# Prompt attention: the scores of four and more key blocks spread over two PSUM banks, the keys' low part through half of the array's rows

## The reference

```python
def window_attend(q, k, v, pos_q, pos_k):
    s = jnp.einsum('...qgrd,...kgd->...qgrk', q, k).astype(jnp.float32) * SCALE
    dpos = pos_q[..., :, None] - pos_k[..., None, :]
    mask = (dpos >= 0) & (dpos < WINDOW) & (pos_k[..., None, :] >= 0)
    s = jnp.where(mask[..., :, None, None, :], s, NEG)
    p = jax.nn.softmax(s, axis=-1)
    return jnp.einsum('...qgrk,...kgd->...qgrd', p.astype(v.dtype), v)
...
        o_cmp, p = cmp_attend(nq, kc, vc, pos_p)
        idx, ok = select_blocks(p, pos_p)
        o_sel = sel_prompt(nq, sk, sv, idx, ok)
        o_win = window_prompt(nq, wk, wv)
        xp = finish(xp, retention_out(ro, rg, ret_gn_w[l]), nsa_combine(gates, o_cmp, o_sel, o_win), *tail)
```

## Time and profile before

| what | value |
|---|---|
| median of 3 runs | 1860.34 us |
| lowest, highest | 1859.66, 1862.49 us |
| profiled execution, its own time | 1858.16 us |
| span of that execution | 1856.3 us |
| PE busy | 1711.2 us (92%) |
| DVE, ACT, POOL busy | 845.9, 619.5, 137.1 us |
| attention of the prompt, on TensorE | about 667 to 968 us of the span |

### The profile page before, as it was taken

How to read it: one execution, slowest core, us unless ns; L and a number is a source line. 1 busy time by engine, 2 the same in 40 slices (tenths; PEclk the granted TensorE clock), 3 DMA queues, 4 the chain that set the end, 5 groups by cost and what they waited for, 6 DMA issues and landing times. The chain is left out here.

```text
span 1856.3 us, 29581 instructions
## 1 busy us (share of the span) xinstructions
PE 1711.2 (92%) x11649; PEld 1516.0 (82%) x11649; DVE 845.9 (46%) x1612; ACT 619.5 (33%) x1193; POOL 137.1 (7%) x236
## 2 busy tenths in 40 slices
PE   3999999994899669999989999999999999999897
PEld 2989989994784555555549889999999999999897
DVE  4466352132016356767876675322332233233366
ACT  5223322210011136666655554201320232023243
POOL 1000000004243300000000110000000000000000
PEclk8999999997899779999999999999999999999899
DMA  7111111125876510000007533211111111111544
GB/s 274 48 47 47 35 47 41 46 57 122 212 211 174 154 29 1 1 1 1 1 17 219 172 117 92 69 46 47 46 46 46 46 52 52 46 46 46 159 132 142
DMA packets 215436, 147.93 MB, mean 80 GB/s; under 512 B 13213, under 2 KB 205090, under 8 KB 214978
## 3 DMA queue, kind: packets, MB, share of 16 engines
q1 hardware_dynamic: 179970, 98.33, 18.8%
q0 software_dynamic: 12288, 37.21, 6.4%
q10 hardware_dynamic: 23040, 10.50, 2.2%
HBM read 133.71 MB, written 16.47 MB: 81 GB/s over the span
## 5 line engine op out<-in xcount | busy, mean ns | idle before, releaser
L1977 PE MATMUL psum<-act_hi,whi 128*128 128x344 f32 x960 | 310.4, 323 | 8.9 <-DVE wlo L2096 5.6
L1977 PE MATMUL psum<-act_hi,wlo 128*128 128x344 f32 x960 | 307.6, 320 | 0.0
L1977 PE MATMUL psum<-act_lo,whi 128*128 128x344 f32 x960 | 307.6, 320 | 0.0
L2096 DVE TENSOR_TENSOR wlo<-wraw,whi 128x1024 fp32r<-128x1024 f32 x111 | 136.0, 1226 | 264.5 <-ACT whi L1993 264.3
L1977 PE MATMUL psum<-hidden_hi,whi 128*128 128x344 f32 x768 | 247.3, 322 | 8.7 <-issue 8.7
L1977 PE MATMUL psum<-hidden_lo,whi 128*128 128x344 f32 x768 | 245.9, 320 | 0.0
L1977 PE MATMUL psum<-hidden_hi,wlo 128*128 128x344 f32 x768 | 245.9, 320 | 0.0
L1993 ACT ACTIVATE whi<-wraw 128x1024 fp32r<-128x1024 f32 x111 | 117.3, 1057 | 349.6 <-PE psum L1977 333.1
L231 PE MATMUL psum<-act_hi,whi 128*128 128x344 f32 x648 | 214.1, 330 | 8.9 <-DVE wlo L263 8.9
L231 PE MATMUL psum<-act_hi,wlo 128*128 128x344 f32 x648 | 207.6, 320 | 0.0
L231 PE MATMUL psum<-act_lo,whi 128*128 128x344 f32 x648 | 207.5, 320 | 0.0
(11 more groups left out here) (369 smaller groups left out, 2473.0 us busy)
## 6 DMA issues: line engine op xcount, KB each, us to landing
wraw<-in_w_down SPq DMA_DIRECT2D x48, 512.0 KB, 3.6
wraw<-in_w_up SPq DMA_DIRECT2D x40, 512.0 KB, 4.0
wraw<-in_w_in SPq DMA_DIRECT2D x27, 512.0 KB, 3.6
wraw<-in_w_o SPq DMA_DIRECT2D x23, 512.0 KB, 4.1
h_features<-mixed_then_h POOLq DMA_DIRECT2D x24, 172.0 KB, 2.4
h_again<-h_features POOLq DMA_DIRECT2D x3, 1376.0 KB, 11.3
x_rows<-in_x_prompt SPq DMA_DIRECT2D x4, 1024.0 KB, 9.6
dec_pages<-in_cache_sel_k SPq DMA_DIRECT2D x64, 64.0 KB, 3.0
```

Source lines behind the costliest of these rows:

```text
L1977: last = pe.matmul(ps[:, u % 3, 0:TN], wt[:, kt, :], xt[:, kt, cols], start=(kt == 0 and i == 0), stop=(kt == KT - 1 and i == 2))
L2096: dve.tensor_tensor(m.wlo[p % 2][:], wraw[raw_slot[p]][:], m.whi[p % 2][:].bitcast(F32), ALU.subtract).then_inc(lo_ready, 1)
```

## The change

Window blocks and selected blocks are treated alike by a new `keys`. With four or more key blocks, the first half of them (rounded up) goes to the end of the first bank, the rest to the start of the second, so that they still lie side by side for the readers (`spare`, `scores`). The high keys go through all 128 rows, once for each bank. The low keys go through 64 rows: bank one through rows 0 to 63, bank two through rows 64 to 127, with the queries' high part alone. The product of the two low parts is thus left out there. As `q_split` has the high part in only one half, `q_other` holds it in the other; GpSimd copies it, twice for each query block. With one to three key blocks nothing changes. In the window of five blocks the oldest and the newest block are taken together as the second bank's part, so one bf16 product of 256 columns adds both masks.

```diff
-        self.causal_bf = self.place("causal_bf", [P, P], BF16, o + 1536)
-        self.winlow_bf = self.place("winlow_bf", [P, P], BF16, o + 1792)
+        self.edges_bf = self.place("window_edges_bf", [P, 2 * P], BF16, o + 1536)
+        self.winlow_bf, self.causal_bf = self.edges_bf[:, 0:P], self.edges_bf[:, P:2 * P]
...
+        q_other = [m.place(f"att_q_other{i}", [P, NH // 2, P], F32R, m.A + 67584 if i else m.stage + 8192) for i in range(2)]
...
+        def window_order(i):
+            lo, hi = window(i)
+            return [lo + 1, lo + 2, lo + 3, lo, lo + 4] if i >= KW - 1 else list(range(lo, hi))
+        def in_first(blocks):
+            return (blocks + 1) // 2 if blocks >= 4 else blocks
+        def spare(blocks):
+            return (4 - in_first(blocks)) * P if blocks >= 4 else 0
+        def scores(bank, blocks):
+            at = spare(blocks)
+            return ps[:, bank:bank + 2, :].rearrange("p a n -> p (a n)")[:, at:at + blocks * P]
...
-            def keys(bank, g, a, w, hi, lo, q):
-                for n, k in enumerate((hi, lo)):
-                    if w == P:
-                        last = pe.matmul(ps[:, bank, 0:2 * P].rearrange("p (a n) -> p a n", n=P), q,
-                                         k[:, g, a:a + P].unsqueeze(1).broadcast_to([P, 2, P]), start=(n == 0), stop=(n == 1))
-                    else:
-                        last = pe.matmul(ps[:, bank, 0:w], q, k[:, g, a:a + w], start=(n == 0), stop=(n == 1))
-                return last
...
+            def keys(bank, g, order, hi, lo, i, h):
+                q, n = q_split[i % 2][:, h // 2, h % 2, :], len(order)
...
+                else:
+                    first = in_first(n)
+                    parts = order[:first], order[first:]
+                    outs = [c.rearrange("p (a n) -> p a n", n=P) for c in (ps[:, bank, (4 - first) * P:4 * P], ps[:, bank + 1, 0:(n - first) * P])]
+                    for part, out in zip(parts, outs):
+                        pe.matmul(out, q, blocks_of(hi[:, g, :], part), start=True, stop=False)
+                    for e, (part, out) in enumerate(zip(parts, outs)):
+                        rows = slice(e * HD, (e + 1) * HD)
+                        q_hi_part = q_split[i % 2][rows, h // 2, e, :] if e == h % 2 else q_other[i % 2][rows, h // 2, :]
+                        pe.matmul(out, q_hi_part, blocks_of(lo[rows, g, :], part), start=False, stop=True)
...
+                    pe.wait_ge(q_moved, 2 * ORDER.index(i) + 2)
...
+                keys(2, g, window_order(i), win_hi, win_lo, i, h)
+                if i >= KW - 1:
+                    last = pe.matmul(ps[:, 3, 0:2 * P], m.ident_bf[:], m.edges_bf[:], start=False, stop=True, skip_group_check=True)
...
+        @block.gpsimd
+        def _(pool):
+            for n, i in enumerate(ORDER):
+                for e in range(2):
+                    rows, other = slice(e * HD, (e + 1) * HD), slice((1 - e) * HD, (2 - e) * HD)
+                    pool.wait_ge(q_hi, 2 * n + e + 1)
+                    pool.tensor_copy(q_other[i % 2][other], q_split[i % 2][rows, :, e, :]).then_inc(q_moved, 1)
```

More of the change, by code:

```diff
@@ new lines, in keys @@
+            def keys(bank, g, order, hi, lo, i, h):
+                q, n = q_split[i % 2][:, h // 2, h % 2, :], len(order)
+                if n == 1:
+                    out = ps[:, bank, 0:2 * P].rearrange("p (a n) -> p a n", n=P)
+                    for x, k in enumerate((hi, lo)):
+                        pe.matmul(out, q, k[:, g, order[0] * P:(order[0] + 1) * P].unsqueeze(1).broadcast_to([P, 2, P]), start=(x == 0), stop=(x == 1))
+                elif n < 4:
+                    out = ps[:, bank, 0:n * P].rearrange("p (a n) -> p a n", n=P)
+                    for x, k in enumerate((hi, lo)):
+                        pe.matmul(out, q, blocks_of(k[:, g, :], order), start=(x == 0), stop=(x == 1))
+                else:
[8 more added lines that the diff above has]
+                        pe.matmul(out, q_hi_part, blocks_of(lo[rows, g, :], part), start=False, stop=True)
@@ L1457, in sel_keys, with at_block @@
+            def at_block(bank, x, n):
+                x += spare(n) // P
+                return ps[:, bank + x // 4, (x % 4) * P:(x % 4 + 1) * P]
             def sel_keys(k):
@@ L1459, in sel_keys @@
                 h = g * R + r
-                q = q_split[i % 2][:, h // 2, h % 2, :]
                 if g == 0 and r == 0:
                     pe.wait_ge(q_lo, 2 * ORDER.index(i) + 2)
+                    pe.wait_ge(q_moved, 2 * ORDER.index(i) + 2)
                 if k:
                     pe.wait_ge(exps, 2 * k - 1)
-                for a in range(0, (i + 1) * P, 512):
-                    keys(a // 512, g, a, min(512, (i + 1) * P - a), sel_hi, sel_lo, q)
-                pe.matmul(ps[:, i // 4, (i % 4) * P:(i % 4 + 1) * P], m.ident_bf[:], m.causal_bf[:], start=False, stop=True,
+                keys(0, g, list(range(i + 1)), sel_hi, sel_lo, i, h)
+                pe.matmul(at_block(0, i, i + 1), m.ident_bf[:], m.causal_bf[:], start=False, stop=True,
                           skip_group_check=True).then_inc(sel_scores, 1)
@@ L1474, in group_blocks @@
                     pe.matmul(ps[:, 3, 256 + x * CP:256 + (x + 1) * CP], q_split[i % 2][:, h // 2, h % 2, :].bitcast(F32), m.kcpT[:, g, :],
-                              start=(i < KW - 1 and x == 0), stop=True, skip_group_check=True)
+                              start=(i < 3 and x == 0), stop=True, skip_group_check=True)
                 return pe.matmul(ps[:, 3, 256:256 + R * CP].rearrange("p (a n) -> p a n", n=CP), m.ident_bf[:],
@@ L1486, in other_keys @@
                     pe.wait_ge(blk_steps, 4 * (k // R) + 2)
[L1487 to L1495, removed]
+                keys(2, g, window_order(i), win_hi, win_lo, i, h)
+                if i >= KW - 1:
+                    last = pe.matmul(ps[:, 3, 0:2 * P], m.ident_bf[:], m.edges_bf[:], start=False, stop=True, skip_group_check=True)
+                else:
+                    last = pe.matmul(at_block(2, i, i + 1), m.ident_bf[:], m.causal_bf[:], start=False, stop=True, skip_group_check=True)
                 if r == 0:
@@ L1522, in output @@
                 n = i + 1 + min(i + 1, KW)
-                lo, _ = window(i)
+                order = window_order(i)
                 if part == 0:
@@ L1535, in output @@
                         x = y - 1
-                        v = m.sv_tok[:, x, rows] if x <= i else m.wv_tok[:, lo + x - i - 1, rows]
+                        v = m.sv_tok[:, x, rows] if x <= i else m.wv_tok[:, order[x - i - 1], rows]
                         last = pe.matmul(out[x % 2], v, pT[grp % 2][:, x, :, :], start=(x == 0), stop=(x >= n - 2))
@@ L1585, in _ @@
                     w = (i + 1) * P
-                    act.activation(p[k % 3][:, 0:w], ps[:, 0:2, :].rearrange("p a n -> p (a n)")[:, 0:w], ACT.Exp,
+                    act.activation(p[k % 3][:, 0:w], scores(0, i + 1), ACT.Exp,
                                    bias=c[:, 1:2], accum_out=c[:, 4:5]).then_inc(exps, 1)
@@ L1591, in _ @@
                     w = min(i + 1, KW) * P
-                    act.activation(p[k % 3][:, SEQ:SEQ + w], ps[:, 2:4, :].rearrange("p a n -> p (a n)")[:, 0:w], ACT.Exp,
+                    act.activation(p[k % 3][:, SEQ:SEQ + w], scores(2, min(i + 1, KW)), ACT.Exp,
                                    bias=c[:, 2:3], accum_out=c[:, 5:6]).then_inc(exps, 1)
@@ L1656, in _ @@
                         dve.wait_ge(scaled, 2 * (k - 2))
-                    dve.tensor_reduce(c[:, 1:2], ps[:, 0:2, :].rearrange("p a n -> p (a n)")[:, 0:(i + 1) * P], AX.X, ALU.max, negate=True).then_inc(maxima, 1)
+                    dve.tensor_reduce(c[:, 1:2], scores(0, i + 1), AX.X, ALU.max, negate=True).then_inc(maxima, 1)
                 if 1 <= k <= len(steps):
@@ L1679, in _ @@
                     dve.wait_ge(win_scores, k + 1)
-                    dve.tensor_reduce(c[:, 2:3], ps[:, 2:4, :].rearrange("p a n -> p (a n)")[:, 0:min(i + 1, KW) * P], AX.X, ALU.max, negate=True).then_inc(maxima, 1)
+                    dve.tensor_reduce(c[:, 2:3], scores(2, min(i + 1, KW)), AX.X, ALU.max, negate=True).then_inc(maxima, 1)
                     if r == 0:
```

7 lines of the change are left out of this document (6 added, 1 removed).

## The result

The changed kernel takes 1868.93 us (median of 6 runs, 1865.86 to 1870.24), the kernel before in the same comparison 1862.37 us (6 runs, 1859.66 to 1864.47). The ratio is 1.0034, 95% interval [1.0021, 1.0047]: slower by 0.34%, some 6.3 us. The forecast was 1865.6 us, slower by 0.28%, range 1857 to 1871. It was built on 1860.34 us for the kernel before, the median of its first three runs; on the 1862.37 us of all six, the same sum would have given 1867.7 us.

The account below looks back on a forecast made before the run. PE was taken to bound the kernel; +4.7 us on PE (selected scores +4.0, window -0.8 and +1.4) and +0.6 for copies made +5.3 on 1860.34, so 1865.6 us, range 1857 to 1871.

Parts of the forecast that it names:

- PE bounds the attention: Attention: PE sets the pace, busy 132.88 of 139.08 us in query blocks 6 to 4; nearly every nanosecond moves the end.
- rival 4: Blocks 7 to 4: PE's waits for ACT absorb 2.6 us of the selected scores' growth; 1863.0 us, chance 0.11.
- do not absorb what is added ahead: Attention: PE's 32 waits for ACT, 11.0 us, start with the transposes and move along with them.
- The halves run together: Score routine: two low products of 64 rows run side by side, the pair costing what its wider half costs.
- rival 3: Score routine: halves run one after the other, +11.4 us more; 1877.0 us, chance 0.07.
- A call pays 0.29: Score routine: changing to half rows and back costs 0.09 + 0.10 + 0.09, plus 0.01, us a call.
- Rival 1: Score routine: the array's shape changes for nothing, 80 calls save 23.2 us; 1842.4 us, chance 0.10.
- rival 2: Score routine: the low pair's load is hidden, only drains cost, 8.0 us less; 1857.6 us, chance 0.08.
- The net by number of blocks: Score calls, net: 8 blocks +0.055, 7 +0.115, 6 +0.105, 5 +0.05, 4 +0.18 us; window of five -0.025.
- The masks: Window, 32 steps: old mask and bared load go, -0.04 - 0.085 us; the wider mask adds +0.05.
- GpSimd's copies: Sixteen copies: fourteen hidden, the first two delay PE's start by 0 to 1.2 us, taken as +0.6.
- their slack hides a copy that delays DVE later: Attention after the start: slack of DVE and ACT hides later copies, so these cost nothing.

Follow-up runs that it names:

- e4: The changed kernel, but both low products of a call go through rows 0 to 63; 1879.86 us, ratio to the kernel before 1.0097.
- e5: The kernel before, plus one product of 64 rows and 64 columns in each of 64 steps, ahead of the window's last mask; 1878.15 us, ratio 1.0087.
- e6: The kernel before, plus one product of 64 columns through all 128 rows in each of 64 steps, same place; 1862.42 us, ratio 1.0003.
- e3: The changed kernel, reordered: low pair first in the selected scores, last after the mask in the window; 1863.13 us, ratio to the kernel before 1.0012.
- e7: The changed kernel with low keys through all 128 rows, no copies, and the oldest block's mask between high and low products; 1857.19 us, ratio 0.9979.
- e1: The changed kernel, but low keys through all 128 rows and no GpSimd copies; 1855.14 us, ratio to the kernel before 0.9966.
- e2: The changed kernel, but four key blocks go as before, in one bank; 1864.88 us, ratio to the kernel before 1.0020.
- e8: The changed kernel with low keys through all 128 rows and no copies, run a second time; 1852.09 us, ratio to the kernel before 0.9955.

## Why the prediction was right

- **PE bounds the attention.** Right. What was added to PE arrived at the end, block by block. PE's wait for the banks of transposes fell from 11.0 us in 32 places to 9.2 in 31, which looks like the sign of rival 4. But by blocks nearly all of the fall (4.19 to 2.63 us) lies in block 7, where the two profiles differ in clock. In blocks 6 and 5 the wait is the same, before and then changed:

```profile
PE psum L1508 <- ACT att_pT L1572: 4.0, 16, 0.3
PE psum L1541 <- ACT att_pT L1613: 4.0, 16, 0.3
```

  So rival 4 is out for blocks 6 and 5. It isn't quite out below them: the forecast's sentence that these waits "do not absorb what is added ahead" fails in four steps of blocks 4 and 3, for 0.35 us together.

- **The halves run together.** Right, by e4; rival 3 is out.
- **A call pays 0.29.** Right: 0.26 to 0.29 in e5 against e6, and 0.09 + 0.20 in the timeline. Rival 1 (nothing) and rival 2 (drains alone, 0.19) are out. The format makes no difference that shows: L538 is fp32 and gave 0.09 and 0.10, the products here are `fp32r`. (For the way back the forecast set 0.43 for a pair of outputs where its own working gives 0.45, so its rows gave 0.07 and not 0.09; e3 finds 0.08.)
- **The net by number of blocks.** Nearly right. At 7 and 6 selected blocks the sum was met within 0.06 us a block. At block 4 it was 0.17 too high and at block 3 0.36 too high. Two things are missing in it. In the two steps of a block in which compressed scores follow the window's mask, the window's scores gain 0.07 to 0.08 us and not the 0.025 forecast: the wider mask costs nothing there. And a part is absorbed ahead of the transposes: in block 4 PE's wait ahead of them shrinks by 0.05 in the second and in the sixth step, in block 3 by 0.09 in the second, and in its fifth step the stretch of the transposes is 0.16 shorter. That fifth step grows from 4.29 to 4.45 us only, where the others of block 3 grow by 0.27 to 0.36.
- **The masks.** Right, and the more interesting half of the change: -0.125 + 0.05 a step, 0.08 to 0.09 by e7.
- **GpSimd's copies.** The forecast's step that failed is "their slack hides a copy that delays DVE later". The size of the first part was right: PE waits 5.80 us for its start and not 5.03, +0.77 where +0.6 was taken, because DVE and POOL stretch each other (DVE's two subtractions take 1.70 us, 1.40 in the earlier trace rows). The rows are from the timeline of the start:

```profile
665.65 1.70 DVE L1645 TENSOR_TENSOR att_q_split<-nqT,att_q_split 64x512 fp32r<-64x512 f32 x2 [0.32 <-ACT att_q_split L1600]
665.68 2.15 POOL L1592 CAST att_q_other<-att_q_split 64x512 fp32r<-64x512 f32 x2 [19.32 <-ACT att_q_split L1600]
667.97 0.77 PE L1486 MATMUL psum<-sel_kT_hi,att_q_split 128*128 128x512 f32 x1 [5.80 <-POOL att_q_other L1592]
```

  But in block 2, where a step is short, a copy also reaches PE: 0.4 us, and nothing had been forecast. In block 1 it is 0.2 more. DVE and POOL in block 2, and what PE waits for two steps later:

```profile
901.66 1.28 POOL L1592 CAST att_q_other<-att_q_split 64x512 fp32r<-64x512 f32 x2 [33.41 <-ACT att_q_split L1600]
```

```profile
902.33 0.83 DVE L1710 TENSOR_SCALAR att_p<-att_p,att_columns 128x384 f32<-128x384 f32 x1
903.08 0.40 DVE L1712 TENSOR_SCALAR att_p<-att_p,att_columns 128x384 f32<-128x384 f32 x1
```

```profile
909.88 0.44 PE L1480 MATMUL psum<-win_kT_hi,att_q_split 128*128 128x384 f32 x1 [1.37 <-ACT att_p L1633]
```

  and the same wait in the kernel before:

```profile
903.48 0.44 PE L1454 MATMUL psum<-win_kT_hi,att_q_split 128*128 128x384 f32 x1 [0.97 <-ACT att_p L1592]
```

  The scaling of 384 columns takes 0.83 us under the copy and 0.42 in the same place of the kernel before. DVE stays 0.41 late, then ACT, then PE. Block 2 takes 29.80 us before and 29.84 in e1, which has no copies, but 30.24 in e2 and 30.27 in e3, which have them. Block 1 shows the same once more, with a scaling of 256 columns that takes 0.70 under a copy and 0.35 before: its length goes from 25.25 us (25.24 in e1) to 25.43 to 25.46 in the four kernels with copies.

- **The total.** Forecast +5.3, measured 6.3 from the ratio, interval 3.9 to 8.8. Blocks 6 to 3 give 3.86, the start 0.77, the waits in blocks 2 and 1 0.4 and 0.2, together 5.2. The rest of 1.1 is not attributed to a part of the change. Block 7 isn't in this sum: its selected calls grow by 0.05 to 0.06 where the clock is 1.00 in both, but PE also waits for exponentials there, and the clock differs. That the total fits so well is partly luck: blocks 6 to 3 came out 0.58 below their forecast of 4.44, and the copies 0.8 above theirs of 0.6.

What stays open is the clock, which the forecast took to be the same on both sides. In the profile of the changed kernel it was low longer in three places: the first block, block 2 behind the longer wait, and the tail, whose code is the same. The first of these isn't bound to half rows, since e7, which has neither half rows nor copies, has 0.77 in its first block too. The second stands only in the changed kernel and in e4 (0.95 in block 2 of both). As a mean over the executions, the granted clock is lowest in the kernels that visit half rows: 0.964 in the changed one (6), 0.966 in e2 and e3 (22), 0.965 in e4 and e5 (8). In e1, e6, e7 and e8 it is 0.967 to 0.969 (36), and 0.967 to 0.968 in the 56 executions of the kernel before beside them. The ranges overlap: e2 alone goes from 0.963 to 0.970. Among those 56, an execution whose clock is 0.001 higher is 0.6 to 1.1 us shorter, so 0.002 to 0.003 of clock is 1 to 3 us (an estimate), as much as what is left over above or more. That it goes with the half rows is a correlation: no experiment changed the clock alone, so it isn't shown that the change lowers it. The block lengths above, all at 1.00, don't depend on it.

## What to carry to other kernels

Count the changes of the array's shape as you count columns: here one visit to half rows costs 0.28 us of TensorE, as much as some 600 columns of `fp32r` at 0.235 us for 512, so a pair of halves pays only if it saves more than that. Next to other work that isn't of full shape one change is paid already, which gave 0.08 back for each in e3; that wasn't enough here. Next to work of its own shape both changes should go, but no run here shows that. A small product of another format between two others can cost more by the load that it lays bare than by its columns; put such products together at the end. And a copy on an idle engine isn't free when it slows an engine that others wait for.

## What was not expected of the hardware

- A product of 64 columns through all 128 rows costs 0.04 us of TensorE in the timeline (776.68 to 776.72), 0.03 a step by the blocks, and 64 of them can't be told from nothing (1.0003 [0.9993, 1.0013]). The same product in half the rows costs 0.32 (0.43 less the 0.11 that the product ahead of it takes).
- DVE's scaling of 384 columns doubled, 0.42 to 0.83 us, under a copy of 64x512 on GpSimd. Two such copies take 1.28 us in block 2 and 2.15 us at the start, where DVE's subtractions run beside them; one has a median of 610 ns and a longest of 1127:

```profile
L1592 POOL CAST att_q_other<-att_q_split x16: 608/610/1127, 665.7 to 933.1; 64x512 fp32r<-64x512 f32 x16
```

The Trainium skill's page "SBUF — State Buffer", section Who interferes with whom, calls the pair of ports that the two engines share an exclusive lock, held for a whole instruction. The trace is in line with it: the scaling starts at 902.33, as the second copy does, and ends 0.22 us after the copies do (901.66 + 1.28 = 902.94). But it loses 0.41 us and not the whole 0.61 of a copy, so the trace doesn't show that one engine stands still for the other's whole instruction.
